# First mixer of a four-block network: feature-major input and output, 1/rms on eviction, layer norm by accumulating passes, chunks in another order

## The reference, cut to what matters

```python
h = rms_norm(x, norm_mix_g[0])            # x * rsqrt(mean(x*x) + eps) * g
z = h @ ab_w_in                           # 1024 x 2560
u, v, gate_b, gate_c, xb = split(z, 512)  # five pieces of 512 columns
u = gelu(u)
v = layer_norm(gelu(v), a_ln_g)           # over 512 features, gain only
mixed = einsum('hts,bcshd->bcthd', tril(a_ws), v) + a_ws_b   # 4 heads, 2 chunks of 128 tokens
y_a = u * mixed
y_b = gate_b * causal_conv(gate_c * xb, b_conv_w)            # 3 taps over tokens
x = x + concat([y_a, y_b]) @ ab_w_out     # 1024 x 1024
# then: MoE layer (32 experts, top 2 of one group), a recurrent mixer, a second
# MoE layer; then a second block with four dense FFNs and two attention mixers,
# and its last FFN adds into the x that is returned
```

## Time and profile before

| | |
|---|---|
| median of 3 runs | 2251.02 us (2249.54 to 2251.11) |
| the profiled execution | 2254.54 us, span in the trace 2252.7 us |
| busy share of the span | TensorE 85%, its weight loads 71%, VectorE 42%, ScalarE 29%, GpSimd 3% |
| chain that ended last, by engine | TensorE 62%, DMA 22%, VectorE 11%, ScalarE 3% |
| read from HBM | 619.5 MB, 275 GB/s over the span |

### The profile page before, as it was taken

The page is one execution under the profiler, slowest core; times in us unless marked ns, Lnnn a source line. Parts: engine busy times, 40 slices in busy tenths (PEclk is TensorE's granted clock), DMA queues, the critical chain, the costliest instruction groups (busy, mean ns, idle before and its releaser), DMA issues.

```text
span 2252.7 us, 35555 instructions
## 1 busy us (share of the span) xinstructions
PE 1922.7 (85%) x16018; PEld 1596.7 (71%) x16022; DVE 949.7 (42%) x1317; ACT 653.0 (29%) x912; POOL 67.0 (3%) x64
## 2 busy tenths in 40 slices
PE   7887776677679867667769999999999999999999
PEld 7863333333478433333439999999999999999999
DVE  4721111111484111111137556756556556666555
ACT  4410000000363000000024445435445444434443
POOL 0000000000000000000000001200000000200000
PEclk9899989989897998998989999999999999999999
DMA  9379999999845999999985554445554554435551
GB/s 382 119 311 426 428 427 427 427 427 427 358 150 217 428 427 428 427 427 427 427 366 179 183 177 167 148 169 171 185 187 169 187 184 155 167 130 191 185 187 57
DMA packets 65278, 622.93 MB, mean 277 GB/s; under 512 B 10848, under 2 KB 11360, under 8 KB 14432
## 3 DMA queue, kind: packets, MB, share of 16 engines
q1 hardware_dynamic: 65120, 620.58, 69.8%
HBM read 619.50 MB, written 1.05 MB: 275 GB/s over the span
## 4 chain that ended last, share of the span: by engine, by line
PE 62%; DMA 22%; DVE 11%; ACT 3%; issue 1%; SPq 1%; DVEq 0%; ACTq 0%
PE ps L451 14%; PE ps L452 14%; PE ps L453 14%; DMA expert_ring_a<-in_moe_w_down 6%; PE ps L663 6%; DMA expert_ring_b<-in_moe_w_down 6%; DMA dense_ring<-in_moe_w_down 6%; PE ps L651 5%; DVE w_lo L1318 3%; PE ps L640 3%; PE ps L900 2%; PE ps L674 2%; DMA expert_ring_a<-in_moe_w_up 2%; DMA dense_ring<-in_dense 2%; ACT w_hi L949 1%
## 5 line engine op out<-in xcount | busy, mean ns | idle before, releaser
L451 PE MATMUL ps<-h_hi,w_hi 128*128 128x256 f32 x2112 | 607.3, 288 | 35.2 <-DVE h_lo L1324 10.9
L1318 DVE TENSOR_TENSOR w_lo<-dense_ring,w_hi 128x1024 fp32r<-128x1024 f32 x384 | 473.5, 1251 | 351.0 <-ACT w_hi L949 350.6
L452 PE MATMUL ps<-h_lo,w_hi 128*128 128x256 f32 x2112 | 602.9, 285 | 0.0
L453 PE MATMUL ps<-h_hi,w_lo 128*128 128x256 f32 x2112 | 602.5, 285 | 0.0
L949 ACT CAST w_hi<-dense_ring 128x1024 fp32r<-128x1024 f32 x384 | 394.5, 1045 | 298.3 <-PE ps L453 284.9
L451 PEld LDWEIGHTS ps<-h_hi,w_hi 128*128 128x128 f32 x2112 | 410.3, 194 | 41.1 <-issue 20.2
L452 PEld LDWEIGHTS ps<-h_lo,w_hi 128*128 128x128 f32 x2112 | 410.7, 194 | 0.1
L453 PEld LDWEIGHTS ps<-h_hi,w_lo 128*128 128x128 f32 x2112 | 410.8, 194 | 0.0
L1587 DVE TENSOR_TENSOR work<-work,ps 128x256 f32<-128x256 f32 x32 | 13.5, 421 | 530.8 <-ACT work L1135 530.8
L451 PE MATMUL ps<-hid_hi,w_hi 128*128 128x256 f32 x704 | 199.7, 284 | 0.6 <-DVE w_lo L1318 0.6
L452 PE MATMUL ps<-hid_lo,w_hi 128*128 128x256 f32 x704 | 199.2, 283 | 0.0
(11 more groups left out here) (277 smaller groups left out, 2065.8 us busy)
## 6 DMA issues: line engine op xcount, KB each, us to landing
dense_ring<-in_dense SPq DMA_DIRECT2D x204, 1024.0 KB, 4.8
expert_ring_a<-in_moe_w_gate SPq DMA_DIRECT2D x24, 2048.0 KB, 31.2
dense_ring<-in_moe_w_up SPq DMA_DIRECT2D x24, 2048.0 KB, 30.7
dense_ring<-in_moe_w_down SPq DMA_DIRECT2D x20, 2048.0 KB, 31.9
expert_ring_b<-in_moe_w_gate SPq DMA_DIRECT2D x20, 2048.0 KB, 31.8
expert_ring_b<-in_moe_w_up SPq DMA_DIRECT2D x20, 2048.0 KB, 34.3
expert_ring_a<-in_moe_w_down SPq DMA_DIRECT2D x20, 2048.0 KB, 33.8
dense_ring<-in_moe_w_gate SPq DMA_DIRECT2D x20, 2048.0 KB, 30.9
```

Source lines behind the costliest of these rows:

```text
L451: mm(o, w[0], x[0], start=start, stop=False, **kw)
L452: mm(o, w[0], x[1], start=False, stop=False, **kw)
L453: return mm(o, w[1], x[0], start=False, stop=stop, **kw)
L1318: V.tensor_tensor(half_of(key, f, 1), tile_of(slot(key), key, f), half_of(key, f, 0).bitcast(F32), ALU.subtract).then_inc(remainder.up(key ...
```

## The change

1. x is laid out by features by the host and loaded in two halves straight into `xT`; the result is stored by features in four quarters straight from `xT`. `entry()`'s transposes and copies and all of `leave()` go.
2. The first mixer gets the scheme that the later mixers have: `gained` writes the rounded x * gain (ScalarE), `less` its remainder (VectorE), products start at once, and 1/rms is applied when PSUM is read: as a per-partition scale in the gelu of v, as a product with `rinv` for u and yb's factor, with `rinv` squared for the gate_c pieces. The sums of squares are made on VectorE for this stage, the mean by `square_mean` after chunk 1, with two more columns that give rms by tokens.
3. Layer norm: the gelu of v is taken in four pieces with an accumulated sum, the variance by two Square passes with bias and accumulated sum on ScalarE; one VectorE instruction per token tile then subtracts and scales. `a_ln_g` moves to the eviction of `mixed`.
4. The order of chunks is v, v, u, u, gate_c, gate_c, xb, xb, gate_b, gate_b. The mask and transposes of `a_ws` come after chunk 3, `mixed` between chunks 8 and 9. `lo` and `hi` of chunk 11 come just ahead of `project`.
5. SP's order: 176 columns of small vectors, chunk 0, x in two halves, chunk 1, constants, chunk 2, `a_ws`, the rest of the small vectors, chunks 3 to 5, one load for all routers, then as before.

```diff
@@ chunk order
-enumerate((2, 3, 6, 7, 8, 9, 4, 5, 0, 1))
+enumerate((2, 3, 0, 1, 6, 7, 8, 9, 4, 5))
@@ TensorE
-        def entry():
-            ... 16 transposes, mean("ab", q)
         def ab():
             for j in range(2):
                 claim(1 + j, acted, "v", j)
                 token_products(("ab", j), 1 + j, "ab")
+            PE.wait_ge(consts_loaded)
+            square_mean("ab", 0)
+            out_of = [("us", 0), ("us", 1), ("gc", 0), ("gc", 1), ("gx", 0), ("gx", 1), ("yb", 0), ("yb", 1)]
+            for j, b in enumerate((3, 4, 5, 6, 7, 1, 3, 4)):
+                claim(b, vec, *out_of[j])
+                tile_products(("ab", 2 + j), b, h_of("ab"))
+                if j == 1:
+                    ... transposes of ws_rows into bank 2
+                if j == 6:
+                    ... 16 matmuls of mixed into banks 0 and 2
+            project("ab", 10, lambda k: (remainder, "y", k // 2))
@@ ScalarE
         def ab():
             hi(("ab", 0))
+            ACT.wait_ge(small_loaded)
+            for q in range(4):
+                gained("ab", q)
             hi(("ab", 1))
+            ACT.wait_ge(consts_loaded)
+            table(ACTF.Sqrt)
+            squares("ab")
+            hi(("ab", 2))
+            rms_later("ab", 0)
+            hi(("ab", 3))
+            ACT.wait_ge(vec, "rinv", "ab")
...
+                    ins = S.activation(v_tok_ab[:, tt, c], bank[1 + j][:, tt * CHUNK:(tt + 1) * CHUNK], ACTF.Gelu_apprx_tanh,
+                                       scale=of_token[:, tt:tt + 1], accum_out=ab_stat[:, 2 * tt + j:2 * tt + j + 1])
...
+                ins = S.activation(ab_cen[:, tt, :], v_tok_ab[:, tt, :], ACTF.Square, bias=ab_stat[:, 4 + tt:5 + tt],
+                                   accum_out=ab_stat[:, 6 + tt:7 + tt])
...
+            for n in (7, 8, 9, 10):
+                hi(("ab", n))
+            for q in range(4):
                 ... rounding of y
+            hi(("ab", 11))
@@ VectorE
-            norm("ab")
+            for q in range(4):
+                less("ab", q)
+            ... lo(1), three sums of squares, lo(2), reciprocal_later, rinv squared, lo(3), mask of ws
+            for j, b in enumerate((3, 4)):
+                ... us(j) = bank * rinv, lo(4 + j)
+            for j, b in enumerate((5, 6)):
+                ... gc(j) = bank * rinv_squared, lo(6 + j)
+            ... v = (v - mean) / std, two instructions
+            for j, b in enumerate((7, 1)):
+                DVE.wait_ge(products, ("ab", 6 + j), 1)
+                ... gx(j), three taps for two groups
+                seq(V.tensor_tensor(pair(ab_acc, j), pair(ab_acc, j), over_tiles(rinv), ALU.mult))
+                lo(("ab", 8 + j))
+            ... yb(0), lo(10), four times (bias and gain, product with u), yb(1), lo_pair of y 0 to 3, lo(11)
@@ SyncE, end
-        for half in range(2):
-            ... store of 512 KB from o_tok
+        for q in range(4):
+            SP.wait_ge(vec, "x", "f21", q)
+            c = slice(q * 2 * T, (q + 1) * 2 * T)
+            sync.dma_start(out[:, c], xflat[:, c]).then_inc(stored.up(q), 16)
```

More of the change, by code:

```diff
@@ L214, in build @@
     probe, _ = place("probe", 1)
[L215 removed]
+    n_route = KD * (N_GROUPS + N_EXP)
+    routers, _ = place("routers", 2 * n_route)
+    w_route = [k_view(routers[:, l * n_route:(l + 1) * n_route], N_GROUPS + N_EXP) for l in range(2)]
     dense, dense_at = place("dense_ring", RING * RING_F)
@@ L574, in ab @@
[L574 to L582, removed]
-            ins.then_inc(products.up("mixed"), 1)
@@ L1437, in ab @@
-            for q in (0, 1):
-                lo_pair(("y", q), h_halves, ab_y, q)
+            sums, less_mean, std, less_std = (ab_stat[:, i:i + 2] for i in (0, 4, 8, 10))
+            for j, b in enumerate((3, 4)):
+                DVE.wait_ge(products, ("ab", 2 + j), 1)
+                V.tensor_tensor(pair(ab_y, j), two(bank[b]), over_tiles(rinv), ALU.mult).then_inc(vec.up("us", j), 1)
+                lo(("ab", 4 + j))
+                if j == 0:
+                    DVE.wait_ge(acted, "v", 1)
+                    parts = ab_stat[:, 0:4].rearrange("p (a j) -> p a j", j=2)
+                    seq(V.tensor_tensor(less_mean, parts[:, :, 0], parts[:, :, 1], ALU.add))
+                    seq(V.tensor_scalar(less_mean, less_mean, -1.0 / D_A, None, ALU.mult), "less_mean")
@@ new lines, in ab @@
+            DVE.wait_ge(products, ("ab", 8), 1)
+            V.tensor_tensor(pair(ab_y, 2), two(bank[3]), pair(ab_acc, 0), ALU.mult).then_inc(vec.up("yb", 0), 1)
+            lo(("ab", 10))
+            DVE.wait_ge(products, "mixed")
+            DVE.wait_ge(rows_loaded)
+            DVE.wait_ge(acted, "u", 1)
+            mixed = view(work, 5632, NA)
+            for h in range(NA):
+                m = bank[h // 2 * 2][:, (h % 2) * T:(h % 2 + 1) * T].rearrange("p (c t) -> p c t", c=TT)
+                bias = small_of("a_ws_b", h * P, P).unsqueeze(1).to_broadcast([P, TT, P])
+                seq(V.scalar_tensor_tensor(mixed[:, h, :].rearrange("p (c t) -> p c t", c=TT), m, small_of("a_ln_g", h, 1), bias,
+                                           ALU.mult, ALU.add))
+                V.tensor_tensor(ab_y[:, h, :], mixed[:, h, :], ab_y[:, h, :], ALU.mult).then_inc(vec.up("ya", h), 1)
```

261 lines of the change are left out of this document (101 added, 160 removed).

## The result

| | before | after |
|---|---|---|
| median of the runs, us | 2251.07 (4 runs, 2249.54 to 2253.4) | 2224.29 (4 runs, 2222.12 to 2225.48) |
| profiled execution / its span, us | 2254.54 / 2252.7 | 2223.39 / 2221.6 |
| first weight product begins | 22.70 | 9.94 |
| chunk 13 multiplied | 123.77 | 100.26 |
| last addition begins / span ends | 2247.33 / 2252.7 | 2218.21 / 2221.6 |

The ratio is 0.9882 with an interval of 0.9870 to 0.9894: the kernel is 26.8 us faster. The forecast was 2227.3 us in a range of 2221 to 2235, that is 23.7 us faster.

What follows compares the result with a forecast made beforehand. Time was taken to follow chunk 13's end, which frees the last slot for the first MoE layer's expert stream, plus the span's last microseconds. Mixer 20.7 and end 3.0 sum to 23.7, from 2251.0 to 2227.3 us, range 2221 to 2235.

Steps and rivals of the forecast that it cites:

- first product: Mixer start: TensorE's first weight product begins at 11.3 us instead of 22.7, 11.4 us earlier.
- hole before `project`: Mixer: TensorE's wait ahead of `project` shrinks to 1.4 us, short enough to leave the clock alone.
- chunk 0 landed: Start: chunk 0, loaded behind 90 KB of small vectors, lands at 5.9 us, bounds 5.0 to 7.0.
- The start: Loads, castings and remainders ahead of the first weight product: it begins 11.4 us earlier, at 11.3 us.
- a table load of 1.28 (to 7.2): ScalarE at the start: a 1.28 us table load after chunk 0's landing at 5.9, before the castings.
- The walk: Mixer, chunk by chunk after the first product: `project` starts at 78.2 instead of 96.73, chunk 13 ends near 103.1.
- The clock behind the hole: Mixer, work after the long hole before `project`: its second half-clock phase costs 2.2 us, which goes too.
- A better start: Rival: chunk 0 at 5.0, a warm array sooner, `mixed` at 1.9; 4 us more gain, 2223 us; chance 0.09.
- VectorE late: Rival: VectorE slips from 56.8 us on, chunks 8 and 9 late, half clock returns; 2232.5 us; chance 0.21.
- Hidden: Rival: something unmoved sets the MoE layer's start, so only the end gains; 2248 us; chance 0.06.
- Slower, by the clock: Rival: TensorE starts from rest and stays at clock 0.5; 2289 us with all 14 chunks cold; chance 0.04.
- The end: Output: two transpose sets fewer ahead of the last addition and a smaller last store give 3.0 us.

Runs made afterwards that it cites:

- run 10: Changed kernel with ScalarE's wait for the small vectors put ahead of the first casting instead of behind it; 2227.18 us, ratio to before 0.9887.
- run 2: Kernel before with only x loaded by features and the new load order, x still ahead of chunk 0, norm before the products; 2247.49 us, ratio 0.9979.
- run 9: Changed kernel with the four router loads of before put ahead of chunk 0; 2225.99 us, ratio to before 0.9883.
- run 1: Kernel before with only the output changed, stored by features in four quarters; 2247.74 against 2251.91 us, ratio 0.9988.
- run 3: Changed kernel with the transposes of `a_ws` and `mixed` put behind chunk 9; median 2230.06 us, ratio to before 0.9900.
- run 4: Changed kernel with the layer norm as a chain on VectorE, as before; 2231.87 us, ratio to before 0.9914.
- run 5: Changed kernel with idle VectorE products ahead of the first remainder of y: 14 (large) gave 2236.8 us, 2 (small) gave 2228.83 us.
- run 7: Changed kernel with 20 warming matmuls and the convolution's two `rinv` products moved to GpSimd; 2222.82 us, ratio to before 0.9875.
- runs 6: Changed kernel with 20 matmuls of zeros into a free bank during the first loads; 2223.53 us, ratio to before 0.9877.

## Why the prediction was right, and where it was off

The sign, the range and both mechanisms (an earlier first product, no long hole before `project`) held; the gain was 3.1 us larger than forecast. Step by step:

| step | forecast | measured after |
|---|---|---|
| chunk 0 landed | 5.9 | 5.94 |
| first product | 11.3 | 9.94 |
| chunks 0 and 1 | 13.9 long | 13.4 |
| `square_mean` | 1.3 | 1.64 |
| transposes of `a_ws` | 1.1 | 0.44 |
| chunk 3 ends | 38.2 | 36.58 |
| `mixed` | 2.5 | 1.95 |
| hole before `project` | 1.4 | 1.7, clock 1.00 |
| `project` begins | 78.2 | 75.21 |
| chunk 13 ends | 103.1 | 100.26 |
| store behind the last addition | 2.6 | 2.7 |
| mixer / end / sum | 20.7 / 3.0 / 23.7 | 23.5 / 2.9 / 26.4 |

**The start** is the term that was most off, by 1.4 us, and its cause is one step: "a table load of 1.28 (to 7.2)". The landing that it was added to was right. The load ran at 0.72 in the wait for chunk 0, and run 10 shows that its cost on the path depends on whether it stands behind a wait: at 6.34 there it costs 1.29 us. The drain that the Trainium skill ("ScalarE: Activation LUTs", What ACT_TABLE_LOAD costs) adds, named in the forecast as 1.4 us more, appears in neither run at the first load. It does not show at a later switch of after either: the load at 27.38 takes 1.28 us and the next activation begins at 28.67. One landing was off without harm: the first half of x came at 8.5 us instead of 7.1 (the queue moved 246 to 358 GB/s in the windows from 2 to 8 us, not the 427 of the forecast), and the first remainder of x still began when VectorE was done with `w_lo`, at 9.32. The 12.8 us divide into 4.6 by the routers and the order behind x (run 2; the routers alone 3.4, run 9), 5.4 by chunk 0 ahead of x, and 2.8 between landing and product by 1/rms on the eviction. Most of the start is the queue. Whether chunk 0 ahead of x would also have helped the old norm, which needs x first, was not tried. The transposes of x, which the forecast counts among what is removed, were hidden by the landing in before.

**The walk** was right in its order. The remaining 1.6 us before `project` are mostly terms that were taken cold where TensorE was warm: the transposes of `a_ws` (0.44 instead of 1.1, more than the clock's factor of 2) and `mixed` (1.95 for 16 matmuls, 0.12 each, so all of it scales with the clock: half of the 3.80 of the earlier trace rows), 1.2 us together, less 0.3 each for `square_mean` and the hole, and half a microsecond in the cold phase at the start, which ended after 3.8 us (13.7). The last half microsecond lies in the length of the chunks. VectorE had one gap of 0.35 us from 54.3 to 75.2, and TensorE waited for it only before `project`, as forecast. Chunk 6 landed near 44.6 instead of 41:

```profile
44.68 2.00 ACT L928 CAST w_hi<-dense_ring 128x1024 fp32r<-128x1024 f32 x2 [4.59 <-DMA dense_ring<-in_dense]
```

It was rounded at once and still in time; of the 5 us to spare, some 1.4 were left.

**The clock behind the hole** was priced at 2.2 us and kept apart from the hole itself. Behind the hole TensorE worked at half clock for 4.5 us in before, but only for 3.1 in run 1, 3.1 in run 3, 4.2 in run 4 and 3.0 in run 5; at 0.21 instead of 0.12 us a matmul that is 1.3 to 1.9 us, so 2.2 was somewhat high. The length at which a hole loses the clock is not a sharp one. Single holes of 1.5 (before, near 77), 1.7, 2.6 (run 7) and 3.1 us (run 5, small) kept 1.00; after the 3.2 us in before, the 4.3 of run 3, the 5.2 of run 4 and the 11.8 of run 5 it was at 0.50. The forecast's "4 us or more" was too generous: before already loses it in 3.2.

**The rivals.** "A better start" (2223) came nearer than the forecast, 1.3 us off against 3.0, on partly other grounds: the warm `mixed` and a somewhat shorter cold phase are its own, the landing at 5.0 did not come (5.94), and the table load, which it doesn't name, gave more than that. "VectorE late" did not occur; run 4, where VectorE is late at an earlier chunk, shows it costing more than the rival's 5.2 us (8.1 at chunk 13, 7.6 between the medians). "Hidden" falls by run 5, and by 23.5 us at chunk 13 that came out at the end. "Slower, by the clock" falls: the cold phase at the start ended 3.8 us after the first product.

**The end** was right to 0.1 us in the profiles (run 1: 3.1), on a ratio that leaves 0.7 to 4.7.

Of the 26.4 us that the two profiles give to mixer and end, 10.0 are the earlier landing of chunk 0, 2.8 the 1/rms on the eviction, 10.7 what happens between the first product and chunk 13, and 2.9 the output. With the mixer of run 1 in place of before's the 10.7 are 9.5. Of them, run 3 gives 7.1 to the place of `mixed`, and run 4 gives 8.1 to the new passes of the layer norm. These two overlap: either edit undone brings a hole back, in another place.

**Open.** Why the stretch behind chunk 13 takes 2116 to 2123 us, and whether the change shortens it. The versions with 20 warming matmuls (runs 6 and 7) have the lowest medians, 2223.53 and 2222.82, but not measurably below after.

## What to carry to other kernels

Follow the first product back to what lands last, and give that load the head of the queue; with the norm's factor applied on the eviction, sending the weights ahead of x was worth 5.4 us here, against 2.8 for the shorter chain itself (the first was not tried with the old norm). Price a hole in TensorE as its length plus 1.3 to 1.9 us of half clock behind it from some 3 us on (3.1 kept the clock, 3.2 did not), and fill it with work whose inputs were made ready earlier on an idle engine. Before a saving of a few microseconds is believed, compare the stretches that the change doesn't touch: here they differed by 4.7 us between two profiles, and the mixer that one edit left alone by 1.5.

## What was not expected of the hardware

- The same load of activation tables costs 0 or 1.3 us, by whether it stands ahead of the first wait (0.72, idle) or behind it (6.34). The Trainium skill ("ScalarE: Activation LUTs", What ACT_TABLE_LOAD costs) counts about 1.38 us of drain beside the load; at this first load the casting follows 0.01 us behind, so no drain shows, and none shows at the switch at 27.38 us.
- The four router loads took up to 3.44 us each to issue behind 2.3 MB of other loads, and 0.42 to 0.73 with only small vectors ahead; there they held the first chunk back by 3.4 us.
- A 128x512 product on GpSimd and a pair of 128x1024 remainders on VectorE side by side took 2.33 and 3.46 us; elsewhere they took 1.3, and 2.36 with GpSimd idle.
- In windows where the granted clock is listed as 1.00, in the first 14 us, matmuls of 256 columns stood 0.21 us apart, and 0.12 after 20 warming matmuls: at the very start the spacing tells more than the listed clock.
